# FFN down groups in seven products per quad, with GpSimd's rows issued behind a sum's load and not behind its landing

## The reference

```python
h2 = rmsnorm(x, norm2_g[l])
g = jnp.einsum('bsd,df->bsf', h2, w_gate[l])
u = jnp.einsum('bsd,df->bsf', h2, w_up[l])
x = x + jnp.einsum('bsf,fd->bsd', jax.nn.silu(g) * u, w_down[l])
...
mod = c_act @ ada_w[l] + ada_b[l]
sh_m, sc_m, g_m, sh_f, sc_f, g_f = jnp.split(mod, 6, axis=-1)
...
y = squared_relu_mlp(h, mlp_up_w[l], mlp_down_w[l])   # square(relu(h @ up)) @ down
x = x + g_f[:, None, :] * rmsnorm_2(y, norm_g[l, 3])
```

## Time and profile before

| | |
|---|---|
| median of 3 runs | 1733.06 us (1732.57 to 1734.9) |
| profiled execution | 1738.16 us, its span 1736.4 us |
| PE | 1714.5 us busy, 99% |
| DVE, ACT, POOL | 1255.6 us (72%), 685.7 us (39%), 119.7 us (7%) |
| HBM read | 231.55 MB, 135 GB/s over the span |

### The profile page before, as it was taken

One profiled execution on the slowest core, in us unless ns is written; L12 is line 12 of the kernel. 1 busy time (PEld: TensorE's weight loads), 2 busy tenths in 40 slices (PEclk: granted clock), 3 DMA queues, 4 the chain that ended last, 5 costly groups with the idle time before them and its releaser, 6 DMA issues. The chain is left out here.

```text
span 1736.4 us, 23695 instructions
## 1 busy us (share of the span) xinstructions
PE 1714.5 (99%) x9000; PEld 1433.3 (83%) x9000; DVE 1255.6 (72%) x1869; ACT 685.7 (39%) x1051; POOL 119.7 (7%) x182
## 2 busy tenths in 40 slices
PE   9999999999999999999999999999999999999998
PEld 8777777888888888888898989887767889898987
DVE  7866555766666676877886878678675887777766
ACT  5236544322222353234534343344534453434341
POOL 0000000011011000100200000002000010000001
PEclk9999999999999999999999999999999999999999
DMA  7321112566566533653264546431411336354541
GB/s 247 111 99 38 49 49 73 194 212 224 193 209 226 193 110 117 230 185 111 63 180 134 167 149 177 163 121 49 139 49 41 106 96 172 97 170 109 161 168 49
DMA packets 67299, 235.77 MB, mean 136 GB/s; under 512 B 7808, under 2 KB 9984, under 8 KB 67008
## 3 DMA queue, kind: packets, MB, share of 16 engines
q1 hardware_dynamic: 46800, 161.24, 27.4%
q0 software_dynamic: 20112, 72.62, 15.1%
q10 hardware_dynamic: 288, 0.59, 0.1%
HBM read 231.55 MB, written 2.10 MB: 135 GB/s over the span
## 5 line engine op out<-in xcount | busy, mean ns | idle before, releaser
L1347 DVE TENSOR_TENSOR w_lo<-w_raw,w_hi 128x1024 fp32r<-128x1024 f32 x307 | 375.3, 1223 | 97.1 <-ACT w_hi L925 90.6
L925 ACT ACTIVATE w_hi<-w_raw 128x1024 fp32r<-128x1024 f32 x307 | 322.6, 1053 | 301.3 <-PE psum L2271 142.8
L2269 PE MATMUL psum<-h_hi,w_hi 128*128 128x512 f32 x1056 | 411.8, 390 | 0.0
L2270 PE MATMUL psum<-h_lo,w_hi 128*128 128x512 f32 x1056 | 410.9, 389 | 0.0
L2271 PE MATMUL psum<-h_hi,w_lo 128*128 128x512 f32 x1056 | 410.8, 389 | 0.0
L2269 PEld LDWEIGHTS psum<-h_hi,w_hi 128*128 128x128 f32 x1056 | 198.3, 188 | 41.8 <-issue 0.5
L2270 PEld LDWEIGHTS psum<-h_lo,w_hi 128*128 128x128 f32 x1056 | 198.3, 188 | 41.4 <-issue 0.5
L2271 PEld LDWEIGHTS psum<-h_hi,w_lo 128*128 128x128 f32 x1056 | 198.2, 188 | 41.2
L1358 DVE SCALAR_TENSOR_TENSOR ada_raw<-ada_raw,c_row 128x1024 f32<-128x1024 f32 x112 | 136.0, 1220 | 8.2 <-DMA ada_raw<-in_ada 8.2
L2269 PE MATMUL psum<-hid_hi,w_hi 128*128 128x512 f32 x344 | 133.8, 389 | 0.0
L2270 PE MATMUL psum<-hid_lo,w_hi 128*128 128x512 f32 x344 | 133.8, 389 | 0.0
(11 more groups left out here) (376 smaller groups left out, 2877.2 us busy)
## 6 DMA issues: line engine op xcount, KB each, us to landing
w_raw<-in_wstream SPq DMA_DIRECT2D x283, 512.0 KB, 4.1
ada_raw<-in_ada POOLq DMA_DIRECT2D x112, 512.0 KB, 3.9
w_diff<-in_wstream SPq DMA_DIRECT2D x12, 512.0 KB, 5.0
w_raw<-in_wstream POOLq DMA_DIRECT2D x12, 512.0 KB, 5.4
w_diff<-in_wstream POOLq DMA_DIRECT2D x12, 512.0 KB, 5.4
x<-in_xT SPq DMA_DIRECT2D x8, 256.0 KB, 5.8
outT<-x SPq DMA_DIRECT2D x16, 128.0 KB, 1.8
con<-in_consts SPq DMA_DIRECT2D x1, 1032.0 KB, 9.7
```

Of the source, the lines that this page charges most:

```text
L925: act.activation(w_hi[:, slot, :], w_raw[:, slot, :], ACT.Copy).then_inc(whi_done, 1)
L1347: dve.tensor_tensor(w_lo[:, slot, :], w_raw[:, slot, :], w_hi[:, slot, :].bitcast(F32), ALU.subtract).then_inc(wlo_done, 1)
L2269: pe.matmul(bank, w_hi[:, slot, w], hi[:, ra + k, :], start=k == 0, stop=False)
L2270: pe.matmul(bank, w_hi[:, slot, w], lo[:, ra + k, :], start=False, stop=False)
```

## The change

The first two FFN down groups become quads, with `x` as their target. The gate-up groups ahead of them make the sums of hidden pairs: after every fourth block VectorE does `pair_sums` and `pair_lo` for two tiles, in place of one low part per tile. Their sums lie in `y`'s room (`pair_sum_ffn`).

GpSimd's `weight_sums` is taken apart into `first_sum` (the accumulating load into `w_raw`) and `last_sum` (that into `w_diff`), without a wait for the landing between them; ScalarE and VectorE wait for `sum_loaded` themselves, and VectorE raises `raw_loaded` behind its split. Rows are issued between the two.

The rows are spread anew. The FFN has 13, 20 and 13 in its gate-up groups and 2 in each of the first two down groups (before: 12, 16, 12 and 12, 12, 0); the first MLP has 8, 8 and 7 in its second, third and fourth up group and 2 in each of its first three down groups (before: 4, 4, 7 and none).

```diff
-            inc.update(gate=nblk // 2, hi=nblk // 2, rhs=nblk // 2)
+            parts = nblk // 4 * 3 if about.get("paired") else nblk // 2
+            inc.update(gate=nblk // 2, hi=parts, rhs=parts, pair=nblk // 4 if about.get("paired") else 0)
...
-            gemm("gateup", 4, "h", h, kouter=AHEAD, summed=summed)
-            gemm("gateup", 12, "h", h, f0=2, rows=12)
+            gemm("gateup", 4, "h", h, kouter=AHEAD, summed=summed, paired=True)
+            gemm("gateup", 12, "h", h, f0=2, rows=13, paired=True)
         else:
-            gemm("gateup", 2 * nk, "h", h, rows=(0, 16, 12)[g])
+            gemm("gateup", 2 * nk, "h", h, rows=(0, 20, 13)[g], paired=g == 1)
...
-        gemm("acc", 8, "hid", hid, nk=nk, dst="x", first=False, sq=False, twin=g == 2, rows=(12, 12, 0)[g])
+        if g < 2:
+            quads(hid, False, "x", 2)
+        else:
+            gemm("acc", 8, "hid", hid, nk=nk, dst="x", first=False, sq=False, twin=True)
...
-    mlp(h, (0, 4, 4, 7), (0, 0, 0, 0), "g_kv", "g_m1", "r_m1", fore=1, old="r_f0", paired=(0, 1, 2))
+    mlp(h, (0, 8, 8, 7), (2, 2, 2, 0), "g_kv", "g_m1", "r_m1", fore=1, old="r_f0", paired=(0, 1, 2))
...
-            def weight_sums(n, k):
-
-                slot = (n + U_A) % RAW
+            def first_sum(n, k):
+
                 pool.wait_ge(sum_begun, 16 * (k + 1))
-                pool.dma_start(w_raw[:, slot, :], wstream[SOURCE[n + U_A][1][1]], accum_op=ALU.add).then_inc(sum_loaded, 16)
-                pool.wait_ge(sum_loaded, 16 * (k + 1))
-                pool.sem_inc(raw_loaded[slot], 16)
+                pool.dma_start(w_raw[:, (n + U_A) % RAW, :], wstream[SOURCE[n + U_A][1][1]], accum_op=ALU.add)\
+                    .then_inc(sum_loaded, 16)
+
+            def last_sum(n, k):
+
                 pool.wait_ge(diff_begun, 16 * (k + 1))
                 pool.dma_start(w_diff[:, :], wstream[SOURCE[n + U_D][1][1]], accum_op=ALU.add).then_inc(diff_loaded, 16)
...
-                    upto = s["at"]["ada"] + s.get("rows", 0) * (s["nblk"] - AHEAD) // (s["nblk"] - 2)
+                    upto = min(s["at"]["ada"] + s.get("rows", 0) * (s["nblk"] - RAW) // (s["nblk"] - 2) + 2, ADA_ROWS)
...
-                    weight_sums(s["at"]["n"] + s["nblk"], s["at"]["quad"])
+                    first_sum(s["at"]["n"] + s["nblk"], s["at"]["quad"])
                 if s["kind"] == "quads":
-                    for q in range(1, QUADS):
-                        weight_sums(s["at"]["n"] + q * QUAD, s["at"]["quad"] + q)
+                    for q in range(QUADS):
+                        if q:
+                            first_sum(s["at"]["n"] + q * QUAD, s["at"]["quad"] + q)
+                        last_sum(s["at"]["n"] + q * QUAD, s["at"]["quad"] + q)
...
+            def split_hi_sum(n, out_wait):
+
+                act.wait_ge(out_done, out_wait)
+                act.wait_ge(sum_loaded, 16 * (SOURCE[n][2] + 1))
+                act.activation(w_hi[:, n % SPLIT, :], w_raw[:, n % RAW, :], ACT.Copy).then_inc(whi_done, 1)
...
-                for m in (n - 1, n - 2 if u == U_B else n - 4):
+                if u == U_B:
+                    dve.wait_ge(sum_loaded, 16 * (quad + 1))
+                for m in (n - 2,) if u == U_B else (n - 1, n - 4):
...
+                    if s["rows"] and u == U_D:
+                        weighted(s["at"]["ada"] + Q, s["at"]["ada"] + Q + 1)
...
-                            lo_of(f)
+                            if not s.get("paired"):
+                                lo_of(f)
+                            elif t.b % 4 == 3:
+                                dve.wait_ge(gu_done, at_["gate"] + f + 1)
+                                pair_sums(s, at_["pair"] + t.b // 4)
+                                pair_lo(s, at_["hi"] + t.b // 4 * 3, (f + s.get("f0", 0)) // 2)
```

More of the change, by code:

```diff
@@ L162, in values, with quads @@
         add("values", dict(n=1, vs=0 if at == 3 else 1, o=4 if at == 3 else 0), group=group, slot=at, rhs="h")
-    def quads(hid, first, dst="y"):
-        add("quads", dict(n=QUADS * QUAD, o=QUADS * QUAD + REST, quad=QUADS), r0=hid, first=first, dst=dst)
+    def quads(hid, first, dst="y", rows=0):
+        add("quads", dict(n=QUADS * QUAD, o=QUADS * QUAD + REST, quad=QUADS, ada=rows), rows=rows, r0=hid, first=first, dst=dst)
     def filler(nblk, chunks, nk, nout, **about):
@@ L260, in mlp @@
             if g in paired:
-                quads(hid, g == 0)
+                quads(hid, g == 0, rows=down[g])
                 continue
@@ L447, in build @@
         y_at = place[0]
+        y_at = place[0]
         y = sb("y", [P, DT, S])
@@ L944, in step @@
                                or isinstance(t.b, int) and t.b < s.get("presplit", 0))
-                    if not nothing:
+                    if s.get("ahead") and t.b == s["nblk"] - 1:
+                        split_hi_sum(t.n + AHEAD, t.o)
+                    elif not nothing:
                         split_hi(t.rounds(AHEAD, RAW), (t.n0 + AHEAD) % SPLIT,
@@ L995, in step @@
                         act.activation(gate, gate, ACT.Silu).then_inc(gate_done, 1)
-                    if evac == "gateup" and t.j % 2 == 1:
+                    if evac == "gateup" and s.get("paired"):
+                        if t.b % 4 == 3:
+                            act.wait_ge(gu_done, at_["gate"] + t.b // 2 + 1)
+                            pair_hi(s, at_["pair"] + t.b // 4, (t.b // 2 + s.get("f0", 0)) // 2)
+                    elif evac == "gateup" and t.j % 2 == 1:
                         act.wait_ge(gu_done, at_["gate"] + t.of(2) + 1)
@@ L1014, in step @@
                                 act.wait_ge(bank_free, BANKS + t.o + 1)
-                                pair_hi(at_["pair"] + t.b // 2, t.b // 2)
+                                pair_hi(s, at_["pair"] + t.b // 2, t.b // 2)
                             return
@@ L1348, in split_lo @@
                                   ALU.subtract).then_inc(wlo_done, 1)
+                if isinstance(m, int) and SOURCE[m][0] == U_A:
+                    dve.sem_inc(raw_loaded[slot], 16)
             def weighted(first, upto):
@@ L1439, in put, with pair_sums @@
                                              op1=ALU.mult).then_inc(bank_free, 1)
-            def pair_sums(p):
+            def pair_sums(s, p):
                 b11, b12, b21, b22 = (scratch[:, i, half_of(h)] for i in range(2) for h in range(2))
-                g3, g2, g4 = (pair_sum[:, i, :] for i in range(3))
+                g3, g2, g4 = (pair_sum_of(s)[:, i, :] for i in range(3))
                 dve.tensor_tensor(g3, b22, b12, ALU.subtract).then_inc(pair_step, 1)
@@ L1648, in step @@
                             dve.wait_ge(out_done, t.o + 1)
-                            dve.wait_ge(rhs_ready, at_["rhs"] + f)
+                            if s.get("paired"):
+                                val = scratch[:, t.b // 2 % 2, :]
+                                dve.wait_ge(rhs_ready, at_["rhs"] + t.b // 4 * 3)
+                            else:
+                                dve.wait_ge(rhs_ready, at_["rhs"] + f)
                             dve.tensor_tensor(val, bank, rstd[:, :], ALU.mult).then_inc(bank_free, 1)
@@ L1661, in step @@
                             dve.wait_ge(bank_free, BANKS + t.o + 1)
-                            pair_sums(at_["pair"] + i)
-                            pair_lo(at_["hi"] + 3 * i, i)
+                            pair_sums(s, at_["pair"] + i)
+                            pair_lo(s, at_["hi"] + 3 * i, i)
                     elif evac == "relu2":
@@ L2799, in lay_out @@
         push(np.stack([gate[c:c + nk], up[c:c + nk]], 1).reshape(2 * nk, P, D))
-        push(tiles(f["w_down"][0][c * P:(c + nk) * P]))
+        down = f["w_down"][0][c * P:(c + nk) * P]
+        push(tiles(down)) if c == 16 else push_quads(down)
     b, c, xh = (tiles(f["conv_in_w_2"][0][:, i * D:(i + 1) * D]) for i in range(3))
```

17 lines of the change are left out of this document (11 added, 6 removed).

## The result

The changed kernel takes **1742.8 us** (median of 6 runs, 1739.4 to 1746.4) against 1733.7 us before: ratio 1.0054, interval 1.0042 to 1.0065. It is 9 us slower. The prediction was 1730.5 us with 1725.5 to 1735.5 as its range, and put a chance of 0.09 on slower. The profiled execution took 1746.4 us, its span is 1744.6.

A forecast was written before the change was run, and what follows sets the result against it. PE, busy 99%, was taken as the bound, with waits at hand-overs from late VectorE and GpSimd. -13.0 + 7.7 + 2.75 = -2.55 us against the profiled 1738.16, taken 5.1 lower to the median: 1730.5 us, range 1725.5 to 1735.5.

The forecast's parts named there:

- What bounds the kernel: Whole kernel: PE, busy 99% of the span, bounds it; time comes only from fewer PE columns, its waits or clock.
- the hand-overs: Start of a seven-product down group: after 36 matmuls (4.32 us) PE wants the last pair's low part from VectorE.
- (a): First two FFN down groups: seven products in place of eight blocks take away 6.43 us, all on PE.
- (b): First MLP's second and third down groups: GpSimd no longer waits for the sum's landing, taking away 6.58 us.
- The first gate-up's wait: Hand-over behind the FFN's first gate-up, 13 rows: PE waits 0.84 us, plus 0.1 added.
- a bound: Rows: 6.2 us from issue to use behind an accumulating load would give over 25 us of added waits.
- The second gate-up's: Hand-over behind the FFN's second gate-up, 20 rows: PE waits 2.93 us, plus 0.1 added.
- The first MLP's: Hand-overs behind the first MLP's second and third up groups, 8 rows: PE waits 1.74 us each, plus 0.1.
- The queues: GpSimd's later `w_diff` operand and ScalarE's own wait for the sum are covered; SP's loads keep the MLP groups' order.
- The clock: PE's clock: one fall counted, 2.75 us, behind the longest stall, with a fair chance of none.
- the fourth: Rival: reload of rows at 4.7 us landing makes the four stalls 13.7 us, 1739.3 us in all; chance 0.08.

The follow-up runs named there:

- experiment 7: Changed kernel with PE filling its waits at the four hand-overs with matmuls whose results nobody reads: 1739.4 us.
- experiment 1: Kernel before with only the GpSimd part (sum issued without waiting for its landing); FFN down groups and rows as before: 1732.7 us, ratio 0.9991.
- 11: Changed kernel with rows moved to where VectorE is idle (10, 14, 14 in the gate-ups, 4 per seven-product group that takes rows): 1728.4 us, ratio 0.9963.
- Experiment 4: Changed kernel with the last row's load ahead of the sum's accumulating load in the two paired gate-ups, GpSimd's order alone: 1740.8 us.
- experiment 3: Changed kernel with rows spread thinner in the FFN's paired gate-ups (10 and 14), 20 in the third, 9 in the MLP's fourth up group: 1740.1 us, ratio 1.0035.
- the second profile: Changed kernel profiled once more without any edit: 1744.8 us.
- experiment 5: Changed kernel with the last row ahead of the sum's accumulating load and a third buffer for the FFN's rows: 1733.6 us, ratio 0.9989.

## Why the prediction was wrong, step by step

The result lies 12.3 us above the forecast. Two steps failed: a gain was read from the profiled execution and taken from the median (5.1 us), and the wait behind the first gate-up was worked out with the median landing of a row, where one row stands behind an accumulating load (4.75 us). Other terms were mis-sized: 1.2 us at the second gate-up, 0.35 in the first MLP, 0.65 for the clock. With the waits as in the profiled execution and the clock as experiment 7 prices it, that makes 12.1 us.

**What bounds the kernel** was right: the hand-overs, and VectorE and GpSimd behind them.

**(a), 6.43 us of PE's time in the FFN,** was right: from experiment 1 to 11 the time falls by 4.3 us, which is 6.4 less the 1.0 us that each of the two hand-overs still costs there (41.31 - 40.31).

**(b), 6.58 us for the GpSimd part,** failed, and this is an error of the sum's frame, not of the mechanism. The profiled execution was 5.1 us above the median, and the stall of 3.34 us with its slow clock was in it. The prediction took (b) from that execution, and then also took the 5.1 us over to the median. Experiment 1 measured 1.5 us. That is 5.1 us too much.

**The first gate-up's wait, 0.84 + 0.1 us,** was 5.69. The price of a row behind an accumulating load was there, as a bound (6.2 us from issue to use), and was set aside because such a row "goes out beside a sum in the last blocks only". But the last blocks are the ones that PE waits for. Experiment 4 gives 4.0 of the 4.75 us to that one row. What it leaves, 1.70 us, is near what the prediction's own working gives with a landing of 4.2 us, the median of this stretch, in place of 3.9: 1.6 us, an estimate. With no double rows either (experiment 3) the wait is 0.72.

**The second gate-up's, 2.93 + 0.1 us,** was 4.24 (3.95 in the second profile): mechanism right, size 1.2 us short. 0.8 of it is again the row behind the sum (experiment 4), and experiment 5 shows that the two buffers' reload is the rest.

**The first MLP's, 1.74 + 0.1 us each,** were 1.88 and 2.15: right. Beside a wait of 0.72 us, a group is 0.28 us longer as PE starts again (41.31 - 40.31 - 0.72); the 0.1 us added for each did not cover that.

**The queues.** No wait of PE on `w_lo` in the profile, and VectorE's wait for the sum's high part (1.65 us) lies within the 2.33 us that the gate's chain takes anyway: right.

**The clock.** One fall was counted, four were there in the profiled execution. The waits of 1.88 and 2.15 us had been counted as harmless. Experiment 7 prices the falls at 3.4 us in the median. That this is not far from the 2.75 counted for one fall is luck. One reading was wrong too: the next longest wait of the profile before is 1.5 us, ahead of PE's first matmul, and not 1.1; nothing in the sum hangs on it.

**The rival that came nearest** was the fourth: the reload, with 1739.3 us. It was priced by a later landing of every row and rejected because the median is 3.9 us. The median after is still 3.9 us; one late row at the end of a group is enough.

With what was measured, from the GpSimd part alone to the changed kernel: -6.4, +9.9 of FFN waits and 0.6 of starts, +3.7 of MLP waits (less the 0.3 that stay), +3.4 of clock, together +11.2; the medians differ by 10.1.

## What to carry to other kernels

Take a gain from the same execution as the time that it is subtracted from: where a profile is longer than the median, what is to be removed may be just that difference. Where one engine must be on time at one point of a group, price the last thing that it waits for there by its own queue's worst row, not by a median over all loads. And work for an idle engine is placed by where its idle time lies: the same 112 rows cost 14 us more in one set of places than in another.
